# A fourth input buffer, two gate blocks kept on chip, smaller weight pieces and a split S5 output in an encoder layer on eight cores

## What is computed

```python
def layer(x, p):
    h = rms_norm(x, g_mix_pre)
    z = h @ w_in                       # u_s | x_c | B_c | C_c | gate_s | gate_c : 1024 x4, 2048 x2
    y = s5_bidirectional(u_s, ...)     # 64 groups of 16 channels, complex state of 64, two directions
    y = gelu(y)
    y = y * sigmoid(y @ w_glu + b_glu)
    y_s = y @ w_s_up                   # 1024 -> 2048
    v = dwconv3(C_c * x_c, conv_w, conv_b)
    y_c = (B_c * v) @ w_c_up           # 1024 -> 2048
    m = sigmoid(gate_s + b_s) * y_s + sigmoid(gate_c + b_c) * y_c
    x = x + rms_norm(m @ w_o, g_mix_post)
    a, b = split(rms_norm(x, g_ffn_pre) @ w_ffn_in)      # 2 x 5632
    return x + rms_norm((silu(a) * b) @ w_ffn_out, g_ffn_post)
```

## Time and profile before

| what | us |
|---|---|
| median of three runs | 1892.12 |
| the profiled execution, its own time | 1890.13 |
| its span on the slowest core (core 4) | 1888.8 |
| spans of the eight cores | 1881.3 to 1888.8 |
| PE busy | 1764.1 (93%), 9616 matmuls |
| DVE busy | 700.0 (37%) |
| ACT busy | 496.0 (26%) |
| front: from the start to own block 1's u-projection | 0 to 86.7 |
| u-projections of own block 1 and far tokens | 86.7 to 162.6 |
| S5 with conv and gates | 162.6 to 684.7 |
| GLU and merge | 684.7 to 845.3 |
| output projection and finish | 845.3 to 981.6 |
| FFN | 981.6 to 1888.8 |

### The profile page before, as it was taken

How to read it: one execution, slowest core, us unless ns; L and a number is a source line. 1 busy time by engine, 2 the same in 40 slices (tenths; PEclk the granted TensorE clock), 3 DMA queues, 4 the chain that set the end, 5 groups by cost and what they waited for, 6 DMA issues and landing times.

```text
span 1888.8 us, 24908 instructions; the slowest of 8 cores (1881.3 to 1888.8 us)
## 1 busy us (share of the span) xinstructions
PE 1764.1 (93%) x9616; PEld 838.7 (44%) x9616; DVE 700.0 (37%) x819; ACT 496.0 (26%) x939; POOL 115.4 (6%) x222
## 2 busy tenths in 40 slices
PE   4799999999997757899999999999999999999998
PEld 2444555544443323344444444444444444444443
DVE  2773888977884643333641101111101110101024
ACT  3652665464544511012440000000000000101010
POOL 0000000000000001110001000000000000000000
PEclk9799999999998879899999999999999999999999
DMA  9563354456668738993545445564645532343456
GB/s 237 159 179 82 66 90 82 76 119 128 116 121 158 167 71 181 191 222 93 179 152 97 81 69 95 91 112 76 104 84 98 87 58 53 62 92 62 90 139 223
DMA packets 85140, 219.03 MB, mean 116 GB/s; under 512 B 34048, under 2 KB 34560, under 8 KB 78208
## 3 DMA queue, kind: packets, MB, share of 16 engines
q0 software_dynamic: 31392, 121.65, 38.7%
q1 hardware_dynamic: 50464, 90.88, 15.6%
q10 hardware_dynamic: 3168, 4.92, 0.7%
HBM read 303.32 MB, written 35.72 MB: 180 GB/s over the span
## 4 chain that ended last, share of the span: by engine, by line
PE 84%; DMA 7%; DVE 4%; issue 3%; ACT 2%; SPq 0%; ACTq 0%; DVEq 0%; POOLq 0%
PE ps L218 83%; DMA wg<-w_in 2%; DMA wr<-w_in 2%; DMA xin<-xseq 2%; DMA yc_d<-ys 1%; DVE Qt L240 1%; PE ps L224 1%; DVE xs L243 0%; DVE Pt L254 0%; DMA xr<-xseq 0%; ACT xs L234 0%; DVE Xt L240 0%; DVE os L243 0%; SPq L212 0%; ACT Xt L234 0%
## 5 line engine op out<-in xcount | busy, mean ns | idle before, releaser
L218 PE MATMUL ps<-hN,wf 128*128 128x512 bf16 x2816 | 608.1, 379 | 0.0
L218 PEld LDWEIGHTS ps<-hN,wf 128*128 128x128 bf16 x2816 | 275.4, 98 | 331.8
L218 PE MATMUL ps<-hT,wr 128*128 128x512 bf16 (+1 forms) x1792 | 344.3, 349 | 17.9 <-ACT ys L236 9.5
L218 PE MATMUL ps<-wfo,agr 128*128 128x512 bf16 x1408 | 304.1, 379 | 0.0
L240 DVE TENSOR_TENSOR agr<-ps,sgt 128x512 bf16<-128x512 f32 x88 | 60.8, 691 | 535.8 <-PE ps L218 535.8
L218 PEld LDWEIGHTS ps<-hT,wr 128*128 128x128 bf16 x1792 | 169.9, 97 | 175.9 <-issue 24.0
L218 PEld LDWEIGHTS ps<-wfo,agr 128*128 128x128 bf16 x1408 | 137.7, 98 | 166.2 <-issue 0.2
L234 ACT ACTIVATE sgt<-ps 128x512 f32<-128x512 f32 x88 | 52.5, 597 | 535.1 <-PE ps L218 535.0
L218 PE MATMUL ps<-wo,mgd 128*128 128x512 bf16 x512 | 113.3, 383 | 1.9 <-DVE mgd L243 1.1
L240 DVE TENSOR_TENSOR facc<-ps,gp2a 128x512 f32<-128x512 f32 x24 | 16.6, 692 | 212.2 <-ACT sqj L234 151.0
L234 ACT ACTIVATE sqj<-ps 128x512 bf16<-128x512 f32 x32 | 19.1, 596 | 270.1 <-PE ps L218 270.1
(11 more groups left out here) (132 smaller groups left out, 1383.2 us busy)
## 6 DMA issues: line engine op xcount, KB each, us to landing
wf<-w_ffn_in POOLq DMA_DIRECT2D x88, 512.0 KB, 6.3
wr<-w_in POOLq DMA_DIRECT2D x48, 512.0 KB, 5.9
...
xin<-xseq SPq DMA_DIRECT2D x16, 1024.0 KB, 7.8
...
yr<-yc_d SPq DMA_DIRECT2D x16, 512.0 KB, 9.8
wo<-w_o POOLq DMA_DIRECT2D x16, 512.0 KB, 16.3
xr<-xseq SPq DMA_DIRECT2D x8, 1024.0 KB, 7.1
```

The source lines that it names most:

```text
L218: return lambda e: e.matmul(o, lhsT=l, rhs=r, start=st, stop=sp)
```

## The change

1. The model's time between engines goes from 0.15 to 0.25 us. This reorders every engine's program.
2. A fourth input buffer (used by tile 3 only), x loads four tiles ahead, seven stages of A ahead of stream S instead of five. `wus` 1 to 7 wait for tile 3's landing instead of tile 1's norm, the S5 sources and the first two `pB` for the norm of tile 5. A Sqrt on one column of a memset stands ahead of all on ACT.
3. `out_stage` has two operations on PE: 32 matmuls that need `Gt` of direction 0, and 16 that need that of direction 1.
4. The gate blocks m = 0 and 2 are computed at D's end, through the ring `wr`, and their tanh is kept in four tiles `hold`; `LATE` has six blocks.
5. `yr` is loaded in 32 halves of 256 KB into seven buffers.
6. `wo` is 16 tiles of 512 KB at places of their own. The one tile lay over `wgl` and part of `gT`, so each of its loads waited for the GLU. Now the four pieces of column block 0 lie where `cv` and `hold` were and wait for nothing else, those of block 1 for four pieces of `g3`, of block 2 for `mgd` 5 to 8, of block 3 for `mgd` 10 to 13.
7. `finish` has one `xg`, and the Square ahead of it leaves its unused output in `xr`'s first half.

```diff
-LATE = (0, 2, 4, 6, 8, 10, 12, 14)
+HELD = (0, 2)
+LATE = (4, 6, 8, 10, 12, 14)
...
-                lat = 0.08 if self.ops[u].eng == e else 0.15
+                lat = 0.08 if self.ops[u].eng == e else 0.25
...
-    XIN = [S.tile("xin%d" % i, [128, D], F32, 35904 + 8192 * i) for i in range(3)]
+    XIN = [S.tile("xin%d" % i, [128, D], F32, a) for i, a in enumerate((35904, 44096, 52288, 197248))]
+    xslot = lambda i: i if i < 4 else (i - 4) % 3
...
+    S.act(small[:, 61:62], small[:, 62:63], AF.Sqrt, 1, [("small", 62)], [("small", 61)])
...
-        if i + 3 < len(tiles):
-            load_x(i + 3)
+        if i + 4 < len(tiles):
+            load_x(i + 4)
...
-        S.dma("pool", flat(wus[:, m, :, :]), w_in[m], 1048576, "wus%d" % m, reads=[("xin1", 0)] if m == 0 else [("small", 1)], writes=[("wus", m)])
-    for i in range(1, 5):
+        S.dma("pool", flat(wus[:, m, :, :]), w_in[m], 1048576, "wus%d" % m, reads=[("xin1" if m == 0 else "xin3", 0)], writes=[("wus", m)])
+    for i in range(1, 7):
         stage_a(i)
...
-        for gq in range(4):
-            o = [bs[hh][0][:, 128 * gq:128 * gq + 128] for hh in range(2)]
-            for hh in range(2):
-                for d in range(2):
+        for d in range(2):
+            items = []
+            for gq in range(4):
...
+            S.mms(items, (ukeys(b) + [("Mst%d" % p, dd, hh) for dd in range(2) for hh in range(2)] if d == 0 else [])
+                  + [("M1_%d" % p, 0), ("M1_%d" % p, 1), ("Gt", d)], [bs[0][1], bs[1][1]])
...
+    HOLD = [S.tile("hold%d" % i, [128, 512], F32, 65728 + 2048 * i) for i in range(4)]
+    for h, m in enumerate(HELD):
+        wg, wgk = wload(w_in[32 + m])
+        for blk in range(2):
...
+            S.act(HOLD[2 * h + blk][:], pg[:], AF.Tanh, 512, [pgk, "hb"], ["hold%d" % (2 * h + blk)], bias=hb[:, m:m + 1], scale=0.5)
...
-        S.dma("sp", yr[:], yc_d[m], 524288, "yr%d" % (m % 4), reads=[("yc_d", m, 0), ("yc_d", m, 1)], writes=[yk])
+        for blk in range(2):
+            yi = (2 * m + blk) % 7
+            S.dma("sp", YR[yi][:], yc_d[m][:, 512 * blk:512 * blk + 512], 262144, "yr%d" % yi, reads=[("yc_d", m, blk)], writes=["yr%d" % yi])
...
-    wo = S.tile("wo", [128, 4, 16, 512], BF16, 97344)
+    at_wo = lambda q: (73920, 78016, 65728, 69824)[q] if q < 4 else 114880 + 4096 * (q - 4)
+    WO = [S.tile("wo%d" % q, [128, 4, 512], BF16, at_wo(q)) for q in range(16)]
...
-                  reads=[("g3", 4 * nb + kq, 0) if nb < 2 else ("mgd", (6 if nb == 2 else 11) + kq, 0)], writes=[("wo", nb, kq)])
+            after = ([], [("g3", kq, 0)], [("mgd", 5 + kq, 0)], [("mgd", 10 + kq, 0)])[nb]
...
-        S.act(xg[:], os_[:], AF.Square, D, OK, [xk, r2k], accum=r2)
+        S.act(xr[:, 0:1024].bitcast(BF16), os_[:], AF.Square, D, OK, ["xr", r2k], accum=r2)
```

More of the change, by code:

```diff
@@ L361, in _program @@
     lam = S.tile("lam_s", [128, 192], F32, 207552)
-    for i in range(3):
+    S.memset(small[:, 62:63], 1.0, [], [("small", 62)])
+    S.act(small[:, 61:62], small[:, 62:63], AF.Sqrt, 1, [("small", 62)], [("small", 61)])
+    for i in range(4):
         load_x(i)
@@ L533, in _program @@
     XS += [S.tile("xs%d" % (2 + i), [128, D], BF16, 197248 + 4096 * i) for i in range(2)]
-    for i in range(5, len(tiles)):
+    for i in range(7, len(tiles)):
         stage_a(i)
@@ L689, in out_stage @@
         bs = [bank("s") for _ in range(2)]
-        items = []
-        for gq in range(4):
-            o = [bs[hh][0][:, 128 * gq:128 * gq + 128] for hh in range(2)]
-            for hh in range(2):
-                for d in range(2):
-                    items.append((o[hh], Mst[p][:, d, hh, gq, :], UB[p][:, 4 * hh + gq, 2:130], d == 0, False, 128))
-            for d in range(2):
+        for d in range(2):
+            items = []
+            for gq in range(4):
+                o = [bs[hh][0][:, 128 * gq:128 * gq + 128] for hh in range(2)]
+                if d == 0:
+                    for hh in range(2):
+                        for dd in range(2):
+                            items.append((o[hh], Mst[p][:, dd, hh, gq, :], UB[p][:, 4 * hh + gq, 2:130], gq == 0 and dd == 0, False, 128))
                 for ri in range(2):
@@ L825, in _program @@
     GK = [("gT", b, g8) for b in range(8) for g8 in range(8)]
-    g3 = S.tile("g3", [128, 8, NTOK], BF16, 179264)
-    YR = [S.tile("yr%d" % i, [128, NTOK], F32, 195648 + 4096 * i) for i in range(4)]
+    g3 = S.tile("g3", [128, 8, NTOK], BF16, 180416)
+    YR = [S.tile("yr%d" % i, [128, 512], F32, 196800 + 2048 * i) for i in range(7)]
     WS = [S.tile("ws%d" % i, [128, 8, 128], BF16, 35904 + 2048 * i) for i in range(5)]
@@ L830, in _program @@
     TS = [S.tile("tsm%d" % i, [128, 512], F32, 54336 + 2048 * i) for i in range(4)]
-    mgd = S.tile("mgd", [128, 16, NTOK], BF16, 64576)
-    GS = [S.tile("gs%d" % i, [128, NTOK], F32, 162880 + 4096 * i) for i in range(2)]
+    mgd = S.tile("mgd", [128, 16, NTOK], BF16, 82112)
+    GS = [S.tile("gs%d" % i, [128, NTOK], F32, 164032 + 4096 * i) for i in range(2)]
     gT2 = gT[:].rearrange("p b i n -> p b (i n)")
```

51 lines of the change are left out of this document (28 added, 23 removed).

## The result

The changed kernel takes 1867.3 us (four runs, 1865.6 to 1868.6), 0.987 of the kernel before with a 95% interval of 0.985 to 0.989. It is 25 us faster, where 56 were forecast. On another chip it was 0.9886 (0.9863 to 0.9908), so this is no accident of one chip. The gain is clear of the noise, but smaller than 2%.

What follows compares the result with a forecast made beforehand. PE, busy 93% of the span, plus its waits in the front, at S5's end and in the merge was taken as the bound. Terms -20 - 24.2 + 4 - 17.3 + 2 = -55.5 gave 1836 us, range 1815 to 1866.

Steps and rivals of the forecast that it cites:

- A, front: Front up to own block 1 and the far tiles: fewer waits for x tiles, block 1 near 72, -20 us (-12 to -25).
- lower bound of -12: Front: only the idle of the named waits goes, 12.9 us, less 1 for new ones.
- early table load: Front, ACT: the table load of 1.28 us goes ahead of the first x tile with the new Sqrt, -1.3 us.
- B, end of S5: S5's end: held gates and the split sum fill waits for `Gt` and `Xt`, -24.2 us, +4 for new small waits.
- what stays is 8.59 for `gT`: Between S5's last sum and the GLU: GELU, store and reload of b = 7 keep PE waiting 8.59 us.
- C, merge: GLU's end to projection: late gate weights no longer awaited, 13.8 us of work moved out, 130.8 to 99.7; gain -17.3 us.
- balance that called the two sides level: Merge: DMA queues need 59.5 + 35.6, 95 us, against PE's 96.7, so neither waits long.
- its alternative for this step: Merge: if halved `yr` loads cost 8 us more DMA time, 103 us against PE's 96.7, gain -13.
- D, finish: Finish: the next `xr` load must wait for ACT's Square, +2 us (0 to +6).
- Rival 2: S5's DVE scan chain takes back the front's gain; GLU starts at 682, time 1860; chance 0.17.
- Rival 4, early half sums: S5: output sums placed ahead of their `Gt` stall PE, about 1900 at 4 us late each; chance 0.03.
- Rival 3: Merge stays short of weights, from two `wo` pieces at D's end and SP's halves; time 1852; chance 0.08.

Runs made afterwards that it cites:

- e_wus: Changed kernel with all `wus` loads triggered by the norm of tile 1 and the fourth input buffer still used once; 0.9802 of the kernel before.
- e_x8b: Changed kernel with the fourth input buffer used for tiles 3 and 7 and all `wus` loads behind the norm of tile 1; 0.9777 of the kernel before.
- e_joined: Changed kernel with the S5 output sum of both directions as one operation again; 0.9883 of the kernel before.
- e_nohold: Changed kernel without held gate blocks, m = 0 and 2 computed in the merge again; 0.9885 of the kernel before.
- e_gtwus: Changed kernel with some `wg`, `ws`, `yr` loads held until the last `gT` loads land, and `wus` behind tile 1's norm; 1848.5 us, 0.9777 of before.
- e_b_split: Kernel before with only the S5 output sum split by direction; 0.9953 of the kernel before.

## Why the prediction was wrong

The time, 1867.3, lies just above the upper end of the range, 1866, and 31 us above the forecast 1836. The span of the profiled execution fell by 21.3 us where the terms add up to 55.5, so 34.2 are missing. By its steps, on the slowest cores:

**A, front: -20 forecast, -4.6 measured.** This is the first step that failed, with 15.4 us. The forecast counted bytes ("about 57 us") and took it that the tiles would be there ("block 1 starts near 72"). It starts at 85.1: tile 8's x lands at 68.3, not near 60, and is then normalised behind tile 9's and S5's table work, 12.8 us from landing to transposes. Behind part of this stands one false wait: tile 5's load waits for a weight block, tile 8's for tile 5's buffer, and the order of ACT and DVE follows from that. I had listed the trigger of `wus` as moved, and never followed what the read of `xin1` did to the next load into that buffer. The runs give back 5.8 us (e_wus, which also starts the weights 4 us sooner) or 7.1 (e_x8b) of the 15.4. For the other 8 no run stands; e_x8b shows where they are, for it starts block 1 at 71.3 and still has the far tokens done only 12.2 us sooner than the kernel before (cores 0 to 3), so the forecast was wrong too that a sooner block 1 moves the far tokens' end by as much. The count of bytes was itself low: 13.3 is in units of 2^20 bytes and 234 GB/s in units of 10^9, and in one unit it is 59 us. The lower bound of -12 was no bound, for it took the removal of the waits for granted. The early table load is there (the first Square starts at 6.93 instead of 9.52), but PE's first transposes come only 0.7 us sooner, at 14.11, because the gains land later than the norm wants them.

**B, end of S5: -24.2 + 4 forecast.** The waits of b = 7 for `Gt` and `Xt` were filled as forecast, and the stall of 9.54 stayed as forecast (9.3): the last sum ends 10.5 us sooner (665.6 for 676.1) with 13.8 us of work added and 4.6 come from the front, so 19.7 were gained, for a forecast of 20.2. The 4 us for new small waits for `Gt` were not needed, since between 186 and 568 PE waits for `wr` alone, 10.5 us. What failed is "what stays is 8.59 for `gT`": it became 20.6, 12 us lost. The step named what follows the last sum, but not what else would be on the DMA engines then. The price was the wrong one of a right chain: it was taken from a moment when they stood idle. And the reason for the filling was half seen: the held blocks do it only together with the split, as e_joined shows, and the changed order does most of it without them, as e_nohold shows.

**C, merge: -31.1 from the GLU's end to the projection forecast, -26.9 measured** (130.7 to 103.8). The mechanism was right, the `wg` wait and `wo` burst are gone; the new small waits are 6.9 (5.1 for `mgd`, 1.8 for `g`) instead of 3. The balance that called the two sides level mixed units as in A: its rates are per 10^6 bytes, its megabytes are of 2^20. In one unit the DMA side is 62 + 38 = 100 us and not 95, above PE's 96.7, and the trace has the DMA engines busy for 0.97 of the 103.8. (From its own figures, 103 us against 130.7, its alternative for this step would have been -14, not -13.)

**D, finish: +2 forecast, +3.4 measured,** within its range, but not for its reason. Of the 3.4 us 2.2 are the first 224 matmuls of the projection (50.6 for 48.3), which run at a granted clock of 0.85 in their first 15 us, behind the wait for `mgd`. The waits for `xg` are one of 2.3, where one of 2.0 was.

**The rivals.** Rival 2 gave about the right time, 1860, and the GLU's start at 682 (measured 686.2), by luck and for a wrong reason: it had S5's DVE chain eat the front's gain, and e_x8b, e_wus and e_gtwus show that a gain in the front arrives at the FFN. Rival 4, early half sums, didn't happen: there is no wait for `Gt` in the list after, and e_b_split even gains. Rival 3 was the closest in kind, a transfer that is late, but at another place.

**The sum.** 15.4 from A, 12.0 from B's `gT` and 0.5 from the rest of B, 0.8 of a slower GLU, 4.2 from C and 1.4 from D are 34.3, for 34.2 missing. e_gtwus removes the collision and the false wait of the front, and lands at 1848.5, 12.5 us above the forecast. What remains is mostly the other 8 of A and the 4 of C.
